# Queries and keys of the second block made with tokens on partitions, then transposed

## Chip, cores and metric

The kernel runs on one core of one Trainium2 chip. The metric is the device time of one execution in microseconds (us). TensorE is PE in the profile, VectorE DVE, ScalarE ACT, GpSimd POOL, and SP issues the weight transfers.

## What is computed

Two blocks of two layers each. The first block's layers are a hybrid mixer, a cross-attention over a memory and a SwiGLU network; the change leaves them alone. The second block takes the first one's output `x` [256 tokens, 1024] and a context of 256 tokens. Its layer has gated branches, one of which is a differential attention: 8 heads with two maps each, every map 64 wide, so queries and keys are 2 x 512 columns each of one large product with the layer's input. For each map of 64 columns `v` of a token, with gain `g`:

```
v = v * rsqrt(mean(v*v) + 1e-6) * g        # queries times 64**-0.5 as well
v = rotate(v, cos, sin)                    # not for the context
```

The rotation pairs columns d and d + 16 within each half of a map, one half by the token's row in a grid 64 wide, the other by its column. Then come scores, two softmaxes, their weighted difference, values, a norm, an output product and a feed-forward network with a small convolution. The context goes through one layer; of its second layer only keys and values are made. `x` goes through two layers and attends to its own tokens and the context's.

## The kernel before

Weights come as 908 units of [128, 1024] fp32, streamed by SP into four slots `raw` (L441). Each is split for exactness: ScalarE rounds it to `whi` (L1030, fp32r), POOL computes the rest `wlo = raw - whi` (L452), and TensorE adds three products (L473 to L475, or L499 to L501). ScalarE rounds the unit four places ahead as soon as TensorE has used the slot (`hi_part`), POOL follows, and SP refills `raw` when POOL is done. All five engines have their order written out by hand, with semaphores between them.

A chunk is 512 output columns over the full depth of 1024: four units. It goes to one of two halves of the PSUM tile `lin`, in one of two layouts. `feature_units` holds a piece of the weights still and streams the 256 tokens: 24 matmuls a unit, features on partitions. `token_units` holds 128 tokens of the input still and streams 512 weight columns: 12 matmuls a unit, tokens on partitions. `after={u: f}` lets TensorE do `f` behind unit u of the chunk.

`second_layer` on TensorE begins with the two chunks of the gated branch, then four chunks of queries (c = 0, 1) and keys (c = 2, 3), all with features on partitions, then two chunks of values with tokens on partitions. After unit 2 of chunk 0 comes `spatial_mix`, eight small fp32 matmuls on the gated branch, which waits for VectorE's statistics and scaling (L2065 to L2076). Four things are done for each chunk c while the next is being made:

- ScalarE evacuates it times the gain to `Z` (L1319, only with rotation) and writes its squares to `probs` (L1320); VectorE multiplies it by the cosines in place (L1933).
- TensorE swaps the partners of the rotation with a permutation matrix (`qk_partners`, L876); VectorE multiplies them by the sines into `probs` (L1476 under L1937), and adds.
- TensorE sums the squares over the partitions of each map (`qk_sums`, L888); ScalarE takes the root, VectorE the reciprocal (L1940), which for queries waits until the softmax.
- For keys TensorE spreads the reciprocals over the partitions (`qk_spread`, L900) and VectorE multiplies by them.

In the next chunk swap and sums stand after unit 0, the spread after unit 1. A pass of its own makes keys and values of the context for the second layer between the context's layer and the first of `x`, with chunks 2 and 3 in the same way. So 14 chunks of queries and keys are made: four in each of three calls, and two. L1476 and L1473 are helpers for every tensor_tensor and copy on VectorE; the tiles tell them apart. On the layer's start VectorE takes two products of the lambda row (L1476) and a sum (L2060).

## Time and profile before

| | us |
|---|---|
| median of 3 runs | 3021.04 |
| lowest, highest | 3016.26, 3025.08 |
| profiled execution | 3019.51 |
| its span | 3017.7 |
| TensorE matmuls busy | 2919.8 |
| POOL busy | 2179.8 |
| ScalarE, VectorE busy | 1515.8, 1097.9 |

Durations of matmul records overlap, since they are pipelined; what a chunk costs is read from stretches of the span. Mean granted clock of TensorE over the span: 0.973 of 2.4 GHz. The second block's layers take up the span from about 1342 us on: the context's layer, its extra pass from about 1863, the layers of `x` from about 1923 and 2478.

### The profile page before, as it was taken

The page shows a single profiled execution, that of the slowest core. Times are in us where ns is not written, and L with a number is a line of the kernel's source. Part 1 is how long each engine was busy: PE and PEld are TensorE (multiplying, and loading weights), DVE is VectorE, ACT ScalarE, POOL GpSimd, SP SyncE. Part 2 cuts the span into 40 slices and gives each one's busy share as a digit, 9 for nine tenths or more (in the row PEclk, how much of TensorE's full clock was granted, in tenths as well). Part 3 has the DMA queues.
Part 4 walks back from the last instruction along what each step waited for, and adds up shares of the span by engine and source line. Part 5 has one row for each costly group of instructions (what it writes and reads, how often), then busy time and mean ns, then how long its engine had stood idle before and what let it go on. Part 6 is the DMA issues. An engine that isn't in the chain of part 4 may idle for free.

```text
span 3017.7 us, 51871 instructions
## 1 busy us (share of the span) xinstructions
PE 2919.8 (97%) x21822; PEld 2692.0 (89%) x21822; DVE 1097.9 (36%) x1976; ACT 1515.8 (50%) x1999; POOL 2179.8 (72%) x912
## 2 busy tenths in 40 slices
PE   7998989999999999999999999999999999999999
PEld 7886969989877969989899999888899999889999
DVE  2411422122313331331552444326534342564433
ACT  4666454445665464454564444445654444465443
POOL 6667788886767688887667786665586866557677
PEclk9999999999999989999999999999999999999999
DMA  6445455555445455554445454533354554434454
GB/s 220 138 153 171 156 179 181 184 189 175 147 154 182 159 191 168 182 197 154 149 149 171 154 186 157 190 129 129 128 174 148 181 182 156 133 126 157 151 182 154
DMA packets 136521, 495.39 MB, mean 164 GB/s; under 512 B 15072, under 2 KB 17760, under 8 KB 135136
## 3 DMA queue, kind: packets, MB, share of 16 engines
q1 hardware_dynamic: 131904, 480.53, 47.6%
q10 hardware_dynamic: 4384, 11.54, 1.1%
q8 instruction: 172, 2.82, 0.4%
q14 instruction: 61, 0.50, 0.1%
HBM read 488.86 MB, written 3.15 MB: 163 GB/s over the span
## 4 chain that ended last, share of the span: by engine, by line
PE 83%; ACT 5%; DVE 4%; POOL 2%; DVEq 2%; issue 1%; ACTq 1%; DMA 1%; SPq 0%
PE lin L473 18%; PE lin L474 17%; PE lin L475 17%; PE aux L473 4%; PE aux L475 4%; PE aux L474 4%; POOL wlo L452 2%; PE lin L499 2%; PE aux L566 2%; PE lin L501 2%; PE lin L500 2%; ACT whi L1030 2%; PE aux L641 1%; PE aux L917 1%; PE lin L616 1%
## 5 line engine op out<-in xcount | busy, mean ns | idle before, releaser
L452 POOL TENSOR_TENSOR wlo<-raw,whi 128x1024 fp32r<-128x1024 f32 x908 | 2179.6, 2416 | 828.6 <-ACT whi L1030 827.4
L1030 ACT ACTIVATE whi<-raw 128x1024 fp32r<-128x1024 f32 x908 | 949.3, 1057 | 975.8 <-PE lin L475 713.8
L473 PE MATMUL lin<-in_hi,whi 128*128 128x256 f32 x3968 | 1146.5, 289 | 25.1 <-POOL wlo L452 22.3
L474 PE MATMUL lin<-in_lo,whi 128*128 128x256 f32 x3968 | 1128.0, 284 | 0.0
L475 PE MATMUL lin<-in_hi,wlo 128*128 128x256 f32 x3968 | 1127.6, 284 | 0.0
L473 PEld LDWEIGHTS lin<-in_hi,whi 128*128 128x128 f32 x3968 | 767.2, 193 | 60.8 <-issue 46.6
L474 PEld LDWEIGHTS lin<-in_lo,whi 128*128 128x128 f32 x3968 | 767.5, 193 | 0.8
L475 PEld LDWEIGHTS lin<-in_hi,wlo 128*128 128x128 f32 x3968 | 766.4, 193 | 0.0
L473 PE MATMUL aux<-br_hi,whi 128*128 128x256 f32 x880 | 249.1, 283 | 0.0
L474 PE MATMUL aux<-br_lo,whi 128*128 128x256 f32 x880 | 249.0, 283 | 0.0
L475 PE MATMUL aux<-br_hi,wlo 128*128 128x256 f32 x880 | 249.0, 283 | 0.0
L473 PE MATMUL lin<-br_hi,whi 128*128 128x256 f32 x768 | 224.8, 293 | 0.0
L474 PE MATMUL lin<-br_lo,whi 128*128 128x256 f32 x768 | 220.4, 287 | 0.0
L475 PE MATMUL lin<-br_hi,wlo 128*128 128x256 f32 x768 | 220.4, 287 | 0.0
L474 PEld LDWEIGHTS aux<-br_lo,whi 128*128 128x128 f32 x880 | 168.9, 192 | 0.0
L475 PEld LDWEIGHTS aux<-br_hi,wlo 128*128 128x128 f32 x880 | 168.9, 192 | 0.0
L473 PEld LDWEIGHTS aux<-br_hi,whi 128*128 128x128 f32 x880 | 168.9, 192 | 0.0
L1846 DVE TENSOR_SCALAR Z<-lin,par_all 128x256 f32<-128x256 f32 x132 | 62.7, 538 | 254.5 <-PE lin L475 254.5
L473 PEld LDWEIGHTS lin<-br_hi,whi 128*128 128x128 f32 x768 | 150.6, 196 | 5.3 <-issue 3.5
L474 PEld LDWEIGHTS lin<-br_lo,whi 128*128 128x128 f32 x768 | 150.7, 196 | 0.2
L475 PEld LDWEIGHTS lin<-br_hi,wlo 128*128 128x128 f32 x768 | 150.4, 196 | 0.0
L1476 DVE TENSOR_TENSOR Z<-Z,lin 128x512 f32<-128x512 f32 (+1 forms) x34 | 29.8, 876 | 293.4 <-ACT Z L1277 264.2
(247 smaller groups left out, 3688.4 us busy)
## 6 DMA issues: line engine op xcount, KB each, us to landing
raw<-in_wstream SPq DMA_DIRECT2D x908, 512.0 KB, 3.3
Z<-in_rel ACTq DMA_DIRECT2D x2, 1536.0 KB, 7.0
Z<-in_mem_t ACTq DMA_DIRECT2D x2, 1024.0 KB, 7.0
kv_store<-Z ACTq DMA_DIRECT2D x2, 1024.0 KB, 6.8
Z<-kv_store ACTq DMA_DIRECT2D x2, 1024.0 KB, 12.7
x<-in_x_t SPq DMA_DIRECT2D x1, 1024.0 KB, 4.9
Z<-in_ctx_t SPq DMA_DIRECT2D x1, 1024.0 KB, 4.9
out_x<-x SPq DMA_DIRECT2D x1, 1024.0 KB, 3.9
```

What stands on the lines that cost most here:

```text
L452: pool.tensor_tensor(wlo[s][:, :], raw[s][:, :], whi[s][:, :].bitcast(F32), ALU.subtract).then_inc(lo_pool, 1)
L473: pe.matmul(out, wh, xh, start=start, stop=False, skip_group_check=True)
L474: pe.matmul(out, wh, xl, start=False, stop=False, skip_group_check=True)
L475: return pe.matmul(out, wl, xh, start=False, stop=stop, skip_group_check=True)
L499: pe.matmul(out, xh, wh, start=start, stop=False, skip_group_check=True)
L500: pe.matmul(out, xh, wl, start=False, stop=False, skip_group_check=True)
L501: return pe.matmul(out, xl, wh, start=False, stop=stop, skip_group_check=True)
L566: mm = pe.matmul(square_sums(b)[:, tt:tt + 1], zt(tiles + k)[:, tt * P:(tt + 1) * P], ones[:, 0:1], start=(k == 0 and tt == 0), stop=(k == ...
L616: pe.matmul(lin[0:4, p, o:o + CH], c, wh[:, w], start=(k == 0), stop=False, skip_group_check=True)
L641: mm = pe.matmul(out, q[:, tt * P:(tt + 1) * P], k[:, 0:(tt + 1) * P], start=True, stop=True)
L1030: act.activation(whi[s][:, :], raw[s][:, :], ACT.Copy).then_inc(hi_ready, 1)
L1846: dve.tensor_scalar(o[c], u[c], w[c][:, 1:2], w[c][:, 3:4], ALU.mult, ALU.add)
```

## The change

All 14 chunks of queries and keys are made with tokens on partitions. ScalarE squares the chunk, VectorE sums the squares of each map (`qk_squares`). With rotation VectorE multiplies the chunk from PSUM by a table of cosines times gain into `y` (two instructions), its exchanged halves by a table of sines times gain into `probs` (four), and adds the two. It takes the reciprocal of the root, and for keys multiplies `y` by it. Without rotation queries are copied and keys are scaled, both from PSUM. After unit 2 of the next chunk TensorE transposes the eight [128, 128] pieces of `y`, and ScalarE evacuates them to the place where features on partitions were (`qk_out`), without rotation times the gain. Swaps, sums and spreads on TensorE go, and so does ScalarE's first evacuation.

The columns of a map come in another order (`ROTATED`), so that rotation partners are 32 columns apart. The tables with the gains are made by eight small instructions of VectorE at the start of a rotating layer (`qk_tables`); the gains come with the lambda row, whose transfer grows from 256 to 512 columns. The wait for the stored keys and values (`kv_sent`) moves from VectorE to ScalarE.

```diff
-C2 = dict(blk=0, perm=128, cos=256, sin=512)
+C2 = dict(cos=0, sin=128, turn=256)
 NC2 = 768
+ROTATED = np.arange(64).reshape(2, 2, 16).transpose(1, 0, 2).reshape(64)
...
-        qk = w[:, QK_COL:V_COL].reshape(D, 2, 2, NH, 64).swapaxes(2, 3).reshape(D, V_COL - QK_COL)
+        qk = w[:, QK_COL:V_COL].reshape(D, 2, 2, NH, 64).swapaxes(2, 3)[..., ROTATED].reshape(D, V_COL - QK_COL)
...
+        def qk_turn(c):
+            return zt(YB + 4 * (c % 2), 4)
+        def qk_table(c, sine, tt):
+            o = C2["turn"] + 256 * (c // 2) + 128 * sine + 64 * tt
+            return c2[:, o:o + 64]
...
+        qk_squares = small[:, 64:80]
...
-            def qk_partners(rotate):
-                if rotate:
-                    pe.wait_ge(qk_raw, t.next(qk_raw))
-                    if t.ahead(qk_done, 0):
-                        pe.wait_ge(qk_done, t.ahead(qk_done, 0))
-                    for h in range(2):
-                        mm = pe.matmul(aux[:, 2 + h, :], c2[:, C2["perm"]:C2["perm"] + P], zt(YB + 2 * h, 2), start=True, stop=True)
-                    mm.then_inc(qk_swap, 1)
-            def qk_sums(rotate, free=None):
-                qk_partners(rotate)
+            def qk_transposes(c, free=None):
+                pe.wait_ge(qk_turned, t.next(qk_turned))
                 if free:
                     pe.wait_ge(free, t.ahead(free))
-                pe.wait_ge(qk_sq, t.next(qk_sq))
                 if t.ahead(qk_done, 0):
                     pe.wait_ge(qk_done, t.ahead(qk_done, 0))
-                for j in range(4):
+                for h in range(4):
                     for tt in range(2):
-                        mm = pe.matmul(aux[:, 0, 4 * j + 2 * tt:4 * j + 2 * tt + 2], probs[:, j * T + tt * P:j * T + (tt + 1) * P],
-                                       c2[:, C2["blk"]:C2["blk"] + P:P // 2], start=True, stop=True)
-                mm.then_inc(qk_ss, 1)
+                        mm = pe.transpose(wide_aux(1 - c % 2)[:, h * T + tt * P:h * T + (tt + 1) * P],
+                                          qk_turn(c)[:, tt * CH + h * P:tt * CH + (h + 1) * P], ident)
+                mm.then_inc(qk_trans, 1)
                 t.skip(qk_done)
-            def qk_spread(c):
-                pe.wait_ge(qk_inverse, t.next(qk_inverse))
-                for j in range(4):
-                    for tt in range(2):
-                        for m in range(2):
-                            r = qk_scale(c)[:, 4 * j + 2 * tt + m:4 * j + 2 * tt + m + 1]
-                            mm = pe.matmul(aux[64 * m:64 * m + 64, j // 2, j % 2 * T + tt * P:j % 2 * T + (tt + 1) * P],
-                                           r.to_broadcast([P, 64]), ident, start=True, stop=True)
-                mm.then_inc(qk_wide, 1)
...
-                feature_chunk(0, after={2: spatial_mix})
+                token_chunk(0, after={2: spatial_mix})
                 for c in range(4):
-                    after = {0: lambda: qk_sums(rotate, ya_ready if c == 0 else None)}
-                    if c > 1:
-                        after[1] = lambda: qk_spread(c)
-                    if c < 3:
-                        feature_chunk((c + 1) % 2, after=after)
-                    else:
-                        token_chunk(0, after=after)
+                    token_chunk((c + 1) % 2, after={2: lambda: qk_transposes(c, ya_ready if c == 1 else None)})
...
-            normed_chunk()
-            feature_chunk(1, after={0: lambda: qk_sums(False), 1: lambda: qk_spread(2)})
-            token_chunk(0, after={0: lambda: qk_sums(False), 1: lambda: qk_spread(3), 3: latent_sums})
+            rms()
+            token_chunk(0, fresh=QUARTERS)
+            token_chunk(1, after={2: lambda: qk_transposes(2)})
+            token_chunk(0, after={2: lambda: qk_transposes(3), 3: latent_sums})
...
-            def qk_chunk(p, c, rotate, first=None, last=None):
-                yield from units(1)
-                if first:
-                    first()
-                yield from units(3)
-                units_done()
+            def qk_chunk(p, roots, last=None, end=None):
+                hi_part()
+                roots()
+                hi_parts(2)
                 if last:
                     last()
-                if rotate:
-                    gain = qk_gain[:, c // 2:c // 2 + 1]
-                    act.activation(zt(YB, 4), lin[:, p, :], ACT.Copy, scale=gain).then_inc(qk_raw, 1)
+                hi_part()
+                units_done()
+                if end:
+                    end()
                 act.activation(probs[:, 0:2 * CH], lin[:, p, :], ACT.Square).then_inc(qk_sq, 1)
 
             def qk_roots():
                 act.wait_ge(qk_ss, t.next(qk_ss))
-                root(qk_root, aux[:, 0, 0:16], qk_std, 1.0 / 64, 1)
-            def values_chunk(p, dst, first=None):
-                hi_parts(1)
-                if first:
-                    first()
-                evacuate(p, 3, dst)
+                root(qk_root, qk_squares, qk_std, 1.0 / 64, 1)
+            def qk_out(c, rotate, side=None):
+                act.wait_ge(qk_trans, t.next(qk_trans))
+                dst = three(zt(Q2 + 4 * c, 4), 4) if c < 2 else key_tiles(c - 2, (0 if rotate else 1) if side is None else side)
+                act.activation(dst, three(wide_aux(1 - c % 2), 4), ACT.Copy,
+                               scale=1.0 if rotate else qk_gain[:, c // 2:c // 2 + 1]).then_inc(qk_done, 1)
...
-                act.dma_start(zt(S2 + 4), a["lam"][l:l + 1, :].to_broadcast([P, T])).then_inc(sgu_landed, 16)
+                act.dma_start(zt(S2 + 4, 2), a["lam"][l:l + 1, :].to_broadcast([P, CH])).then_inc(sgu_landed, 16)
...
-                run(qk_chunk(0, 0, rotate, value_std, lambda: input_hi(br_hi[:, 0:4 * T], wide_aux(0))))
+                qk_chunk(0, value_std, None, lambda: input_hi(br_hi[:, 0:4 * T], wide_aux(0)))
+                v = VL if rotate else VC
                 for c in range(1, 4):
-                    run(qk_chunk(c % 2, c, rotate, qk_roots))
-                v = VL if rotate else VC
-                if rotate and l == 0:
-                    act.wait_ge(kv_sent, t.next(kv_sent, 32))
-                values_chunk(0, zt(v, 4), qk_roots)
+                    if c == 3 and rotate and l == 0:
+                        act.wait_ge(kv_sent, t.next(kv_sent, 32))
+                    qk_chunk(c % 2, qk_roots, lambda: qk_out(c - 1, rotate))
+                hi_part()
+                qk_roots()
+                hi_parts(2)
+                qk_out(3, rotate)
+                evacuate(0, 1, zt(v, 4))
...
+            def maps(ap, tt):
+                return ap[:, tt * CH:(tt + 1) * CH].rearrange("p (n d) -> p n d", d=64)
+            def part(ap, tt, s):
+                return ap[:, tt * CH:(tt + 1) * CH].rearrange("p (n s d) -> p n s d", s=2, d=32)[:, :, s]
+            def over_maps(ap, n):
+                return ap.unsqueeze(1).to_broadcast([P, 8, n])
+            def qk_tables(l):
+                gains = zt(S2 + 5)
+                for i in range(2):
+                    for sine in range(2):
+                        for tt in range(2):
+                            o = C2["sin" if sine else "cos"] + 64 * tt
+                            dve.scalar_tensor_tensor(qk_table(2 * i, sine, tt), c2[:, o:o + 64], (64 ** -0.5, 1.0)[i],
+                                                     gains[:, 128 * i + 64 * sine:128 * i + 64 * sine + 64], ALU.mult, ALU.mult)
+                settle()
+            def qk_chunk(c, rotate, between=None):
+                p = c % 2
+                z, y, b = lin[:, p, :], qk_turn(c), probs[:, 2 * CH:4 * CH]
+                scale = qk_scale(c).unsqueeze(2).to_broadcast([P, 16, 64])
                 if between:
                     between()
                 dve.wait_ge(qk_sq, t.next(qk_sq))
+                dve.tensor_reduce(qk_squares, probs[:, 0:2 * CH].rearrange("p (n d) -> p n d", d=64), AX.X, ALU.add).then_inc(qk_ss, 1)
+                if t.next(qk_done) > 2:
+                    dve.wait_ge(qk_done, t.ahead(qk_done, -2))
                 if rotate:
-                    dve.scalar_tensor_tensor(z, z, gain, over(cos, 4), ALU.mult, ALU.mult)
+                    for tt in range(2):
+                        tt_(maps(y, tt), maps(z, tt), over_maps(qk_table(c, 0, tt), 64), ALU.mult)
+                    for tt in range(2):
+                        for s in range(2):
+                            i = tt_(part(b, tt, s), part(z, tt, 1 - s), over_maps(qk_table(c, 1, tt)[:, 32 * s:32 * s + 32], 32), ALU.mult)
+                    i.then_inc(lin_free[p], 1)
                     settle()
-                if rotate:
-                    dve.wait_ge(qk_swap, t.next(qk_swap))
-                    tt_(turned, three(wide_aux(1), 4), over(sin, 4), ALU.mult)
+                    tt_(y, y, b, ALU.add)
                     settle()
                 dve.wait_ge(qk_std, t.next(qk_std))
-                i = dve.reciprocal(qk_scale(c), qk_root)
-                if c > 1:
-                    i.then_inc(qk_inverse, 1)
-                if rotate:
-                    tt_(dst, z, turned, ALU.add).then_inc(lin_free[p], 1)
-                else:
-                    dve.tensor_scalar(dst, z, gain, None, ALU.mult).then_inc(lin_free[p], 1)
-                settle()
-                if c > 1:
-                    dve.wait_ge(qk_wide, t.next(qk_wide))
-                    tt_(dst, dst, three(wide_aux(0), 4), ALU.mult)
-                settle().then_inc(qk_done, 1)
+                dve.reciprocal(qk_scale(c), qk_root)
+                settle()
+                if rotate and c > 1:
+                    tt_(y.rearrange("p (n d) -> p n d", d=64), y.rearrange("p (n d) -> p n d", d=64), scale, ALU.mult)
+                elif c > 1:
+                    tt_(y.rearrange("p (n d) -> p n d", d=64), z.rearrange("p (n d) -> p n d", d=64), scale, ALU.mult).then_inc(lin_free[p], 1)
+                elif not rotate:
+                    copy(y, z).then_inc(lin_free[p], 1)
+                settle().then_inc(qk_turned, 1)
...
+                    qk_tables(l)
...
-                    if c == 2 and rotate and l == 0:
-                        dve.wait_ge(kv_sent, t.next(kv_sent, 32))
```

## Rows read from the trace of the kernel before

**Rows 1.** the page, part 1: busy time, share of the span and instructions of each engine

```profile
PE 2919.8 (97%) x21822; PEld 2692.0 (89%) x21822; DVE 1097.9 (36%) x1976; ACT 1515.8 (50%) x1999; POOL 2179.8 (72%) x912
```

**Rows 2.** groups by form on TensorE (line engine op names shapes xcount | busy us, mean ns)

```profile
L888 PE MATMUL aux<-c,probs 128*128 128x2 f32 x224 | 25.9, 246 | 0.5 <-DVE br_lo L1476 0.5
L900 PE MATMUL aux<-c,qk_inv 128*64 128x128 f32 x256 | 15.7, 276 | 0.0
L876 PE MATMUL aux<-Z,c 128*128 128x512 f32 x32 | 15.2, 598 | 0.5 <-ACT Z L1319 0.5
```

**Rows 3.** windows (from:to, length, busy us of PE PEld DVE ACT POOL, PEclk, DMA share, GB/s)

```profile
1935.08:1945.99 10.91, 10.91 (x51) 9.02 (x49) 4.49 (x3) 5.16 (x5) 10.91 (x5) 1.00 0.76 272
1983.18:1994.78 11.60, 11.60 (x99) 11.60 (x99) 1.33 (x2) 5.03 (x6) 6.61 (x4) 1.00 0.38 123
1979.76:1983.18 3.42, 3.42 (x23) 2.46 (x21) 2.52 (x2) 1.31 (x2) 2.94 (x2) 1.00 0.62 205
2001.24:2003.13 1.89, 1.89 (x33) 1.72 (x32) 0.00 (x0) 1.06 (x1) 0.59 (x1) 1.00 0.01 2
2200.53:2202.25 1.72, 1.72 (x16) 1.72 (x17) 0.00 (x0) 1.70 (x2) 1.72 (x1) 1.00 0.83 293
1945.99:2025.52 79.53, 77.47 (x593) 70.57 (x592) 28.01 (x31) 32.94 (x36) 49.79 (x22) 1.00 0.43 144
2500.50:2577.97 77.47, 77.22 (x593) 70.51 (x592) 24.99 (x31) 32.94 (x36) 47.84 (x21) 1.00 0.42 142
1365.23:1436.13 70.90, 70.39 (x577) 67.48 (x576) 15.06 (x23) 29.33 (x32) 47.98 (x21) 1.00 0.46 154
```

**Rows 4.** groups by form on VectorE

```profile
L1476 DVE TENSOR_TENSOR probs<-aux,c 128x1024 f32<-128x1024 f32 x8 | 9.8, 1225 | 1.2 <-PE aux L876 0.9
L1476 DVE TENSOR_TENSOR br_lo<-aux,br_hi 128x256 fp32r<-128x256 f32 x32 | 13.6, 424 | 149.0 <-ACT br_hi L1087 149.0
L1476 DVE TENSOR_TENSOR Z<-Z 128x1024 f32<-128x1024 f32 x8 | 26.6, 3322 | 1.1 <-issue 0.5
L1476 DVE TENSOR_TENSOR Z<-Z,small 128x1024 f32<-128x1024 f32 x6 | 13.7, 2329 | 0.2
L2038 DVE TENSOR_REDUCE small<-probs 128x2 f32<-128x256 f32 x24 | 10.1, 422 | 2.0
L1940 DVE RECIPROCAL qk_inv<-qk_inv 128x16 f32<-128x16 f32 x14 | 3.5, 253 | 61.1 <-ACT qk_inv L1054 61.1
```

**Rows 5.** timeline of POOL and of VectorE (start us, us, engine line op names), 308 to 317

```profile
307.51 5.28 POOL L452 TENSOR_TENSOR wlo<-raw,whi 128x1024 fp32r<-128x1024 f32 x2 [0.48 <-ACT whi L1030]
...
310.51 3.37 DVE L1476 TENSOR_TENSOR Z<-Z 128x1024 f32<-128x1024 f32 x1
```

**Rows 6.** timeline of ScalarE, 1976.9 to 1985.5

```profile
1977.14 1.06 ACT L1030 ACTIVATE whi<-raw 128x1024 fp32r<-128x1024 f32 x1 [1.82 <-PE lin L475]
1979.10 1.02 ACT L1320 ACTIVATE probs<-lin 128x1024 f32<-128x1024 f32 x1
```

**Rows 7.** windows, as in Rows 3, at two waits of TensorE and behind them

```profile
1490.00:1492.60 2.60, 0.01 (x1) 0.00 (x0) 1.22 (x5) 2.44 (x6) 0.13 (x1) 1.00 0.00 0
1492.60:1496.00 3.40, 2.87 (x21) 2.30 (x22) 3.19 (x6) 1.01 (x2) 3.40 (x2) 1.00 0.13 13
2085.20:2088.10 2.90, 0.07 (x1) 0.00 (x0) 1.75 (x5) 2.44 (x6) 0.36 (x1) 1.00 0.01 3
2089.10:2092.50 3.40, 3.40 (x13) 2.05 (x10) 3.12 (x5) 0.34 (x1) 3.32 (x2) 0.50 0.40 131
```

**Rows 8.** timelines of POOL and VectorE, starts of the second block's rotating layers

```profile
1932.38 26.36 POOL L452 TENSOR_TENSOR wlo<-raw,whi 128x1024 fp32r<-128x1024 f32 x11 [5.01 <-ACT whi L1030]
...
1939.59 2.35 DVE L1476 TENSOR_TENSOR small<-par_all,c 128x1 f32<-128x1 f32 x1
1948.28 1.29 DVE L2065 BATCH_NORM_STATS2 small<-Z 128x6 f32<-128x512 f32 x2 [5.98 <-ACTq L1374]
...
2502.79 1.29 DVE L2065 BATCH_NORM_STATS2 small<-Z 128x6 f32<-128x512 f32 x2 [17.38 <-ACTq L1374]
```

More of the change, by code:

```diff
@@ L501, in token_product, with token_units @@
                 return pe.matmul(out, xl, wh, start=False, stop=stop, skip_group_check=True)
-            def token_units(p, src=None, after=()):
+            def token_units(p, src=None, after=(), fresh=()):
                 xh, xl = src or (in_hi, in_lo)
@@ L506, in token_units @@
                 for k0 in range(0, KD, 2):
+                    if k0 in fresh:
+                        pe.wait_ge(inputs_ready, t.next(inputs_ready))
                     wh, wl = next_unit()
@@ L1440, in _ @@
             rms(context, True)
-            run(qk_chunk(0, 2, False))
-            run(qk_chunk(1, 3, False, qk_roots))
+            qk_chunk(0, lambda: None)
+            latent_square(0)
+            qk_chunk(1, qk_roots, lambda: qk_out(2, False, 0))
             hi_part()
+            latent_square(1)
             qk_roots()
-            for q in range(3):
-                latent_square(q)
-                hi_part()
+            hi_part()
+            latent_square(2)
+            hi_part()
+            qk_out(3, False, 0)
             latent_square(3)
-            evacuate(0, 0, zt(VL, 4))
+            evacuate(0, 1, zt(VL, 4))
             norm_root(0, 1)
@@ L2212, in shape_constants @@
 def shape_constants():
-    i = np.arange(P)
     c1 = np.zeros((P, NC1), np.float32)
@@ L2269 @@
     taps = taps.reshape(L, 4, 2, NCH, 2, P).transpose(0, 5, 3, 2, 4, 1).reshape(L, P, 16 * NCH)
-    twice = [np.concatenate([v[n], v[n]], -1)[:, :, None] for n in ("q_norm_g_2", "k_norm_g_2")]
+    gains = [v[n][:, ROTATED] for n in ("q_norm_g_2", "k_norm_g_2")]
+    twice = [np.concatenate([g, g], -1)[:, :, None] for g in gains]
     par2 = np.concatenate([tiles(v["norm1_g_2"]), tiles(v["norm2_g_2"]), tiles(v["sgu_ln_g_2"])] + twice
@@ L2280 @@
         sgu_w=v["sgu_w_2"].transpose(0, 3, 1, 2).reshape(L * P, CH), sgu_b=v["sgu_b_2"].reshape(L, CH),
-        lam=np.concatenate([v[n] for n in ("lam_q1_2", "lam_q2_2", "lam_k1_2", "lam_k2_2")], -1),
+        lam=np.concatenate([v[n] for n in ("lam_q1_2", "lam_q2_2", "lam_k1_2", "lam_k2_2")]
+                           + [w for g in gains for w in (g, np.roll(g, 32, -1))], -1),
     )
```

34 lines of the change are left out of this document (13 added, 21 removed).

## Prediction

> **What bounds the kernel now.** I read first the busy line of the page [rows 1]: TensorE's matmuls fill 97% of the span, POOL 72%, the other two half or less. What TensorE is given to do is therefore the time, as long as nobody makes it wait. Next, who makes it wait, in the view of waits: in the part that changes only the spatial mix of one layer waits to speak of, and that stretch has 2.06 us idle in 79.53 [rows 3]. Then the price of each kind of TensorE work in that part, by form [rows 2] and by stretch [rows 3]. Last, the helpers, since the change moves work to VectorE, which shares something with POOL [rows 4, 5].
>
> **Price of a chunk.** A chunk of four units takes TensorE 10.91 us when made with tokens on partitions and 11.60 with features on partitions; the second starts behind a group of small matmuls, which costs it 0.08 [rows 3]. So 0.69 a chunk, 0.155 a unit.
>
> **What leaves TensorE.** The swaps (L876), square sums (L888) and spreads (L900) count 32, 224 and 256 matmul records [rows 2], at 4, 16 and 32 a group: 8, 14 and 8 groups. A swap with a sum takes 3.42 us [rows 3]; halved, 1.71 each. A spread takes 1.89. Together 22 x 1.71 + 8 x 1.89 = 52.7 us, all on the path, as TensorE is full there.
>
> **What comes.** Eight transposes a chunk, 14 chunks. Sixteen of the same kind take 1.72 us [rows 3]; eight 0.86, and 0.15 for the matmuls to start again behind them: 14 x 1.01 = 14.1. Bounds: 0.8 and 1.9 a group (the dearest small group in [rows 3]).
>
> **Check by stretch.** From the first query chunk to the last key chunk's end plus one value chunk the second and third layer calls take 79.53 and 77.47 us, the context 70.90 [rows 3]. Anew, each is five token chunks (54.55), a spatial mix (1.71, as a sum) and four transpose groups (4.04): 60.3. That gives 19.2, 17.2 and 10.6. The context's pass for the second layer's keys loses two sums and two spreads and turns two chunks: 3.4 + 3.8 + 1.3, restarts 0.5, less 2.0, is 7.0. Sum 54.0. The parts give 52.7 + 14 x 0.69 - 14.1 = 48.3; the stretches add the idle time of before (2.06, 0.25 and 0.51, busy time against length [rows 3]) and some 0.1 us of restart behind each of the 30 small groups, 3. **Gross saving 54.0 us**, if TensorE never waits.
>
> **Where it will wait.** TensorE asks for a chunk's transposes when three units of the next are done: 3 x 2.73 = 8.2 us after the chunk's own end, T. What must happen by then, from T: ScalarE rounds one unit, then squares; in the trace, where T is 1979.76 - 2.88 = 1976.9, the rounding starts at T + 0.2 and the squares at T + 2.2, with an evacuation of 1.0 between that now goes [rows 6]. So the squares run from 1.2 to 2.2. VectorE sums 1024 columns: 1.2, from 0.42 for 256 [rows 4]. Then two products of 512 and four of 256 columns. These read one operand from PSUM; 1024 columns take 1.23 and 256 take 0.42 [rows 4], so 2 x 0.6 + 4 x 0.33 with their overlap: 2.6. At T + 6.0 the sum y + b wants to start, with everything in SBUF.
> This is the weak step. Instructions of VectorE with both inputs in SBUF are dear in this trace: 3.32 us against 1.23 for the same 1024 columns [rows 4]. One is shown [rows 5]: it starts while POOL works, and ends 1.08 us after that POOL instruction (307.51 + 5.28 = 312.79) has ended. POOL's takes 2.40 [rows 8]. So they take turns. POOL's instructions follow ScalarE's rounding of the units at T + 0.2, 2.9 and 5.7, hence run from 1.4, 4.1 and 6.8. The sum lands in the second, waits to 6.5, ends at 7.6; with the reciprocal (0.25 [rows 4]) and drains, ready at 8.0. **Query chunk 1: no wait.** A key chunk has a second such instruction, the scaling. POOL has taken its turn at 7.6 and holds to 9.9; the scaling ends at 11.0. **Key chunks: 2.9 us each.** Chunk 0 starts 1.3 later, as ScalarE and VectorE first do the gating tile; its sum comes at 7.3, meets POOL's third (to 9.2), ready at 10.7: **2.5 us**. Each layer that rotates: 2.5 + 0 + 2.9 + 2.9 = 8.3; two: 16.6. In the context and its second pass there is no rotation and the scaling reads PSUM: ready by T + 6.7, no wait. Bounds for one chunk: 0 (nothing waits for POOL; the chain ends by 8.8) and 5.5 (one turn more).
>
> **The tables.** Eight small products a rotating layer, both inputs in SBUF, before the gates' statistics. In the first such layer POOL runs eleven instructions without a gap from 1932.38 [rows 8], and VectorE's single-column product there takes 2.35 us: a turn each. From 1942.3 five tables wait a turn (2.5 each, to 54.4); then POOL runs dry, because ScalarE waits for the statistics with its rounding behind it, and the rest is quick. The statistics start at 55.0 for 48.28 [rows 8], the mix at 58.4, where TensorE is ready at 54.2: 4.2 us idle (the 2.06 of before is in the stretch's saving already). In the last layer VectorE has 17.38 us idle there [rows 8], which hides six or seven turns: 0. Bounds 0 and 8 over both.
>
> **The clock.** A wait of 2.9 us is followed by 3.4 us at 0.50 of the clock, that is 1.2 GHz; another of 2.6 is not [rows 7]. Half of 3.4 at half speed costs 1.6 to 1.7. Of the seven waits above (4.2, 2.5 twice, 2.9 four times) I charge six: 9.8. Bounds 0 and 16.
>
> **Costed at nothing.** ScalarE's new evacuations (1.0 a chunk) fall between the third and fourth unit, with units already rounded ahead; without that lead each would cost its 1 us. The wait for kv_sent moves to ScalarE, with the transfer long landed. The lambda row grows from 1 to 2 KB a partition behind two transfers as large. Weights, SP's queue and POOL's work are the same: POOL needs 2.40 a unit, TensorE 2.73.
>
> **Sum.** The profiled execution took 3019.5 us (span 3017.7), 1.5 under the median of 3021.0. 3019.5 - 54.0 + 16.6 + 4.2 + 9.8 = 2996.1 against its own time; for a median 1.5 more, **2997**.
>
> **What a page adds.** Sixteen transposes at 2200.53 ran at clock 1.00 between dense matmuls [rows 3]. The Trainium skill, "TensorE: Matmul & The Clock Gate", Part 4, says that transpose-mode work does not count as busy for the clock. By that rule a drop would follow each of the 14 groups; nothing in [rows 3] shows it for 1.72 us between full stretches. What it would give is the second rival.
>
> **Rivals.**
> *No turns.* The new SBUF instructions slip between POOL's: y + b and scaling 1.2 each. Chunk 0 and the keys wait 0.7, the tables nothing, no clock drop: 3021 - 54 + 4 + 2 = 2973. For: POOL idles 0.48 before its instructions [rows 5]. Against: the six instructions of the scaling's form average 2.33, the eight of the sum's 3.32 [rows 4]. 0.15.
> *A clock drop at every group*, or a turn more for chunk 1 and in the last layer's tables: 14 x 1.65 instead of 9.8, or 2 x 2.5 + 3 + 3 drops: about 3010. For: groups of low activity follow waits. Against: [rows 3]. 0.15.
> *The rotation itself waits in turn.* If the six products with a table in SBUF were held by POOL as well, nine turns would stand in a chunk's chain. POOL has at most four instructions in hand before TensorE stalls (four slots), so the chain ends at 1.4 + 4 x 2.4 + 6.2 = 17.2, a wait of 9. Eight chunks: 72, clock 13, tables 4: 3021 - 54 + 89 = 3056, slower. It decides from about 6 us of loss a chunk. Against: products of that form take 1.23 whether POOL runs or not [rows 4]. 0.06.
> *TensorE's saving is no saving* because units come no faster (POOL or transfers bound): 3015 to 3021. Against: a token chunk takes 10.91 with POOL at work all through it [rows 3]. 0.05.
>
> **Numbers.** Forecast 0.59. About 0.3% (9 us) is what a measurement of this kernel can tell from no change: the forecast, the first and the second rival lie below 3012. The range leaves out the third and fourth and the ends of the others: 2975 to 3012. Faster 0.86, same 0.08, slower 0.06.
>
> **What would show it.** In the profile after: three or more lines gone (swaps, sums, spreads), 112 transposes at some 0.11 us pace; token chunks at 10.9; idle of TensorE before the transposes near 16.6 us in 6 or 7 pieces, released by VectorE's scaling or reciprocal; VectorE's y + b at 1.5 to 3.5 us each; a wait of 4 us before the first rotating layer's mix; six short stretches at half clock. The step most likely wrong is the chain on VectorE; if TensorE's idle time there is under 5 us the first rival holds, if over 60 the third.

## The result, and the profile after

| | before | after |
|---|---|---|
| median, us | 3019.42 (4 runs, 3016.26 to 3025.08) | 2991.08 (4 runs, 2988.91 to 2997.06) |
| profiled execution, its span | 3019.51, 3017.7 | 2991.71, 2989.9 |
| mean granted clock | 0.973 | 0.971 |

The ratio is 0.9911, 95% interval 0.9896 to 0.9925: 28 us off, where 24 were forecast (2997 from a median of 3021.04; range 2975 to 3012). The page's busy line after the change, beside [rows 1]:

```profile
PE 2873.9 (96%) x20750; PEld 2627.2 (88%) x20750; DVE 1149.2 (38%) x2030; ACT 1521.4 (51%) x2005; POOL 2189.0 (73%) x912
```

TensorE has 46 us less to do, VectorE 51 more, POOL 9 more. In the groups by form the swaps, sums and spreads of [rows 2] are gone and 112 transposes have come (L890; line 900 is now the spatial mix). The idle time before them stands behind the second bar.

```profile
L890 PE MATMUL aux<-c,Z 128*128 128x128 f32 x112 | 16.8, 299 | 16.1 <-DVEq L1965 16.1
L900 PE MATMUL aux<-Z 128*128 128x128 f32 x48 | 7.4, 321 | 3.3 <-DVE Z L2092 3.3
```

Now windows (columns as in [rows 3]). First a token chunk of the context's layer, with the restart behind a group; a group of eight transposes; then the stretches that answer to the last three of [rows 3], context, first and last layer that rotate: 59.92 for 70.90, 78.04 for 79.53, 70.42 for 77.47.

```profile
1387.36:1398.35 10.99, 10.99 (x52) 9.05 (x51) 2.70 (x3) 5.83 (x7) 8.82 (x5) 1.00 0.47 161
1398.35:1399.14 0.79, 0.79 (x9) 0.79 (x8) 0.00 (x0) 0.53 (x1) 0.79 (x1) 1.00 1.03 342
1365.65:1425.57 59.92, 59.92 (x291) 50.19 (x289) 17.85 (x25) 33.08 (x36) 49.25 (x21) 1.00 0.54 182
1926.44:2004.48 78.04, 66.94 (x289) 55.17 (x288) 44.30 (x58) 32.81 (x36) 55.05 (x22) 0.91 0.46 153
2479.35:2549.77 70.42, 62.14 (x291) 51.05 (x289) 37.73 (x52) 33.04 (x36) 53.70 (x21) 0.98 0.48 164
```

The context's layer saves 11.0, as TensorE is never idle there. The layers that rotate would save as much and more, and give it back in idle time (11.1 and 8.3 us: length less PE busy) and in clock (0.91 and 0.98). The view of waits names the two lines that are new:

```profile
PE aux L890 <- DVEq L1965: 16.1, 6, 2.9
PE aux L900 <- DVE Z L2092: 3.3, 1, 3.3
```

Six waits before the transposes of chunks 0, 2 and 3 of both layers, none before chunk 1's, none in the context. What holds VectorE is seen in the timeline of a key chunk (start us, us), VectorE's rows first, then two of POOL's instructions:

```profile
1975.49 1.28 DVE L1468 TENSOR_TENSOR Z<-lin,c 128x512 f32<-128x512 f32 x2
1976.69 1.41 DVE L1468 TENSOR_TENSOR probs<-lin,c 128x256 f32<-128x256 f32 x4
1978.19 1.53 DVE L1468 TENSOR_TENSOR Z<-Z,probs 128x1024 f32<-128x1024 f32 x1
1979.80 0.25 DVE L1957 RECIPROCAL qk_inv<-qk_inv 128x16 f32<-128x16 f32 x1
1980.12 2.90 DVE L1468 TENSOR_TENSOR Z<-Z,qk_inv 128x1024 f32<-128x1024 f32 x1
```

```profile
1976.23 2.41 POOL L462 TENSOR_TENSOR wlo<-raw,whi 128x1024 fp32r<-128x1024 f32 x1 [0.33 <-ACT whi L1016]
1978.93 3.01 POOL L462 TENSOR_TENSOR wlo<-raw,whi 128x1024 fp32r<-128x1024 f32 x1 [0.29 <-ACT whi L1016]
```

POOL's first ends at 1978.64 and the sum y + b 1.08 us later; its second ends at 1981.94 and the scaling, asked for at 1980.12, 1.09 later, at 1983.03. The turn is taken both ways: POOL's second instruction, which started while the sum was at work, took 3.01 us, the one before it 2.41. The six products that read one operand from PSUM (`lin`) run at their own pace beside POOL.

**Where the time went.** For each profiled execution I count three things from the first matmul to the last: TensorE's idle pieces of over 1 us, what stretches at 0.50 of the clock cost (half their length), and the rest.

| | idle | half clock | rest | median of runs |
|---|---|---|---|---|
| before | 53.5 | 80.2 | 2862.3 | 3019.42 |
| after | 70.7 | 87.0 | 2810.4 | 2991.08 |

So 52.0 us of work left TensorE, 17.2 came back as idle time and 6.8 as clock; what remains is the 27.9 by which the stretch from first to last matmul is shorter. The rest is the steady part: in the experiments below in which TensorE's work is that of the changed kernel it lies between 2808 and 2815, while the half-clock column moves by up to 20 us, most of it in stages that no edit touches (the first block alone has from 44 to 56 us of it).

### The profile page after: what moved, and what is told of

Its sections match the earlier page's. It is cut to its first block, busy times and chain, and to the rows that moved or that the text cites. A ratio compares the mean times of both kernels' runs of the same rounds, so it can differ in the third digit from the quotient of the medians.

```text
span 2989.9 us, 49777 instructions
## 1 busy us (share of the span) xinstructions
PE 2873.9 (96%) x20750; PEld 2627.2 (88%) x20750; DVE 1149.2 (38%) x2030; ACT 1521.4 (51%) x2005; POOL 2189.0 (73%) x912
## 4 chain that ended last, share of the span: by engine, by line
PE 82%; DVE 6%; ACT 5%; DVEq 2%; POOL 2%; issue 1%; ACTq 1%; DMA 1%; SPq 0%
PE lin L483 16%; PE lin L484 16%; PE lin L485 16%; PE aux L483 4%; PE aux L485 4%; PE aux L484 4%; PE lin L509 3%; PE lin L511 3%; PE lin L510 3%; ACT whi L1016 2%; PE aux L578 2%; POOL wlo L462 2%; PE aux L908 1%; PE aux L653 1%; DVE Z L1468 1%
## 5 line engine op out<-in xcount | busy, mean ns | idle before, releaser
L483 PE MATMUL lin<-in_hi,whi 128*128 128x256 f32 x3520 | 1018.1, 289 | 24.5 <-POOL wlo L462 22.9
L484 PE MATMUL lin<-in_lo,whi 128*128 128x256 f32 x3520 | 1001.4, 284 | 0.0
L485 PE MATMUL lin<-in_hi,wlo 128*128 128x256 f32 x3520 | 1001.1, 284 | 0.0
L483 PEld LDWEIGHTS lin<-in_hi,whi 128*128 128x128 f32 x3520 | 681.2, 194 | 59.5 <-issue 46.1
L484 PEld LDWEIGHTS lin<-in_lo,whi 128*128 128x128 f32 x3520 | 681.5, 194 | 0.6
L485 PEld LDWEIGHTS lin<-in_hi,wlo 128*128 128x128 f32 x3520 | 680.6, 193 | 0.0
L509 PE MATMUL lin<-whi,in_hi 128*128 128x512 f32 x464 | 186.3, 402 | 0.1
L511 PE MATMUL lin<-whi,in_lo 128*128 128x512 f32 x464 | 182.5, 393 | 0.0
L510 PE MATMUL lin<-wlo,in_hi 128*128 128x512 f32 x464 | 182.5, 393 | 0.0
```

Of the source, the lines that this page charges most:

```text
L483: pe.matmul(out, wh, xh, start=start, stop=False, skip_group_check=True)
L484: pe.matmul(out, wh, xl, start=False, stop=False, skip_group_check=True)
L485: return pe.matmul(out, wl, xh, start=False, stop=stop, skip_group_check=True)
L509: pe.matmul(out, xh, wh, start=start, stop=False, skip_group_check=True)
L510: pe.matmul(out, xh, wl, start=False, stop=False, skip_group_check=True)
L511: return pe.matmul(out, xl, wh, start=False, stop=stop, skip_group_check=True)
```

## Experiments

Theory: on VectorE an instruction with both operands in SBUF takes turns with POOL's (it waits for POOL's to end, and POOL's for it), whatever its size; that makes the six waits and the mix's wait. Rivals: the chain of instructions is too long by itself; or transposes lower the clock. Each diff is against the changed kernel; L numbers are lines of the kernel that ran. Ratios are to the kernel before, with 95% intervals.

**1. The sums in PSUM** (`e1_sums_in_psum`). The same arithmetic; `b` lies in a free half of `aux`, and for keys so does the sum that the scaling reads.

```diff
-                z, y, b = lin[:, p, :], qk_turn(c), probs[:, 2 * CH:4 * CH]
+                z, y, b = lin[:, p, :], qk_turn(c), wide_aux(1 - c % 2)
-                    tt_(y, y, b, ALU.add)
+                    tt_(b if c > 1 else y, y, b, ALU.add)
...
-                    tt_(y.rearrange("p (n d) -> p n d", d=64), y.rearrange("p (n d) -> p n d", d=64), scale, ALU.mult)
+                    tt_(y.rearrange("p (n d) -> p n d", d=64), b.rearrange("p (n d) -> p n d", d=64), scale, ALU.mult)
```

> The sine products go to PSUM instead of SBUF, and for keys the sum too, so that neither the sum nor the scaling has both inputs in SBUF; number and columns of VectorE's instructions stay. Theory (VectorE's instructions with two SBUF inputs take turns with POOL): sums and scalings take about 1.2 us each instead of 1.9 and 2.9, TensorE's idle time before the transposes falls from 16.1 to about 3.5 us (0.5 for chunk 0, 0.6 for each key chunk), the half-clock stretches of this part fall from five to one or two, and the time from 2991 to about 2972. Rival (the chain on VectorE is simply too long, whoever else works): nothing changes, 2991.

Median 2971.0, ratio 0.985 (0.9833 to 0.9866), 20 us under the changed kernel by the medians, 18 by the ratios. Its view of waits, and two rows of VectorE's timeline in a key chunk, which POOL's instruction from 1970.32 to 1972.70 overlaps:

```profile
PE aux L890 <- DVEq L1965: 4.6, 6, 1.1
```

```profile
1969.59 1.23 DVE L1468 TENSOR_TENSOR aux<-Z,aux 128x1024 f32<-128x1024 f32 x1
1971.22 1.22 DVE L1468 TENSOR_TENSOR Z<-aux,qk_inv 128x1024 f32<-128x1024 f32 x1
```

The scaling went from 2.90 to 1.22 us, the waits from 16.1 to 4.6, and none of the six was followed by a half-clock stretch. As many instructions, in the same order: it is not the chain's length.

**2. The transposes one unit later** (`e3_after_unit_3`), the sums left in SBUF.

```diff
-                    token_chunk((c + 1) % 2, after={2: lambda: qk_transposes(c, ya_ready if c == 1 else None)})
+                    token_chunk((c + 1) % 2, after={3: lambda: qk_transposes(c, ya_ready if c == 1 else None)})
...
-                    qk_chunk(c % 2, qk_roots, lambda: qk_out(c - 1, rotate))
+                    qk_chunk(c % 2, qk_roots)
+                    qk_out(c - 1, rotate)
...
+                evacuate(0, 1, zt(v, 4))
                 qk_out(3, rotate)
-                evacuate(0, 1, zt(v, 4))
```

ScalarE's evacuation of the transposes so comes behind its squares; on VectorE nothing is edited.

> The transposes of a chunk stand after unit 3 of the next chunk instead of unit 2, 2.7 us later, and ScalarE evacuates them after its squares; no instruction's operands change. Theory: the sums keep their 1.5 to 3 us and the scalings 2.9, but the chain, ready 8.4 to 10.9 us after the chunk's end, now meets a deadline of 10.9: TensorE's idle time there falls from 16.1 to under 1.5 us, four half-clock stretches go, 2970. Rival (the wait only moves: the evacuation comes later and holds up the next chunk's buffer, the first scores or the units' rounding): 2985 to 2995 with TensorE idle elsewhere.

Median 2969.96, ratio 0.9844 (0.983 to 0.9859). Of the waits at L890 one of 0.2 us is left, though by form VectorE's instructions are dearer than in the changed kernel (1909 and 2902 ns there):

```profile
L1469 DVE TENSOR_TENSOR Z<-Z,probs 128x1024 f32<-128x1024 f32 x8 | 21.6, 2694 | 0.7
L1469 DVE TENSOR_TENSOR Z<-Z,qk_inv 128x1024 f32<-128x1024 f32 x4 | 11.8, 2938 | 0.3
```

The turns cost only because TensorE asked 2.7 us too early. Two quite different edits give about the same: 18 and 20 us by the ratios.

**3. Two columns** (`e4_tiny_sbuf`, `e5_tiny_psum`). A product of 2 columns, needed by nobody, behind chunk 1's reciprocal and ahead of the signal; in the second kernel its first operand is `wide_aux(0)[:, 0:2]`, in PSUM.

```diff
+                if rotate and c == 1:
+                    tt_(small[:, 84:86], qk_squares[:, 0:2], qk_squares[:, 0:2], ALU.mult)
```

> One more VectorE product of two columns, both inputs in SBUF, behind the reciprocal of query chunk 1 in the two rotating layers (its result is not used). Theory (a turn, whatever the size): it takes about 2 us instead of 0.2, chunk 1's transposes, which had no wait, wait about 2 us in each layer; 4 us more, up to 7.5 with half-clock stretches: 2995 to 2999. Rival (its own size counts): 0.2 us each, 2991.

> The same added product of two columns as in the run with the tiny product, but one of its two operands comes from PSUM. Theory (turns with POOL for an instruction with both operands in SBUF): about 0.1 to 0.3 us each instead of 1.83, no wait before chunk 1's transposes, so five waits of 2.4 to 3.0 us and the short one at line 890, some 16 us in all, time 2989 to 2993. Rival (any further product in that place costs what the other one did, its own start and end): about 1.8 us again, with waits of 1.6 us before chunk 1's transposes.

VectorE's product and POOL's instruction beside it, first with both operands in SBUF, then with one in PSUM:

```profile
1962.39 1.84 DVE L1468 TENSOR_TENSOR small<-small 128x2 f32<-128x2 f32 x1
1961.22 2.99 POOL L462 TENSOR_TENSOR wlo<-raw,whi 128x1024 fp32r<-128x1024 f32 x1 [0.31 <-ACT whi L1016]
```

```profile
1965.22 0.16 DVE L1468 TENSOR_TENSOR small<-aux,small 128x2 f32<-128x2 f32 x1
1964.05 5.36 POOL L462 TENSOR_TENSOR wlo<-raw,whi 128x1024 fp32r<-128x1024 f32 x2 [0.31 <-ACT whi L1016]
```

The same two columns, the same place in the chain, and POOL at work in both: 1.84 us, ending 0.02 behind POOL's end, against 0.16, with 1.68 of POOL's instruction (the first of the two in its row, which ends at 1967.06) still to run. The second rotating layer has the same two numbers within 0.01. With the first TensorE got two more waits, of 1.61 us each, before chunk 1's transposes (line 890: 19.0 us in 8), with the second none (15.8 in 6). The times do not show it: 2990.49 (0.9919, 0.9898 to 0.994) and 2985.86 (0.9897, 0.9872 to 0.9922). The intervals overlap, and the first, forecast at 2995 to 2999, is no slower than the changed kernel: its profiled execution had 8.5 us less of half clock, by chance as far as I can see, and its two new waits were followed by none. The price of the turn is shown by the rows, that of the wait only in the trace.

The Trainium skill, "SBUF — State Buffer", section on the two sides of SBUF, says that a VectorE instruction with two SBUF inputs and a GpSimd instruction that reads SBUF exclude one another for the whole instruction. These rows agree, down to 2 columns, and so does experiment 1 for the remedy.

**4. The tables in four instructions** (`e2_tables_split`): two of 128 columns before the statistics, two behind chunk 0's sum, instead of eight of 64 before.

```diff
-            def qk_tables(l):
+            def qk_tables(i):
                 gains = zt(S2 + 5)
-                for i in range(2):
-                    for sine in range(2):
-                        for tt in range(2):
-                            o = C2["sin" if sine else "cos"] + 64 * tt
-                            dve.scalar_tensor_tensor(qk_table(2 * i, sine, tt), c2[:, o:o + 64], (64 ** -0.5, 1.0)[i],
-                                                     gains[:, 128 * i + 64 * sine:128 * i + 64 * sine + 64], ALU.mult, ALU.mult)
+                for sine in range(2):
+                    o, g = 128 * sine, gains[:, 128 * i + 64 * sine:128 * i + 64 * sine + 64]
+                    two = lambda c: c2[:, c:c + 128].rearrange("p (t d) -> p t d", t=2)
+                    dve.scalar_tensor_tensor(two(C2["turn"] + 256 * i + o), two(o), (64 ** -0.5, 1.0)[i],
+                                             g.unsqueeze(1).to_broadcast([P, 2, 64]), ALU.mult, ALU.mult)
                 settle()
...
-                    qk_tables(l)
+                    qk_tables(0)
...
                 for c in range(4):
                     lo_parts(4)
                     qk_chunk(c, rotate, gating_lo if c == 0 else None)
+                    if rotate and c == 0:
+                        qk_tables(1)
```

> Two table instructions before the gates' statistics instead of eight (the key tables are made after chunk 0, when VectorE is idle; each instruction does both halves of the tokens). Theory (each costs one POOL instruction of 2.4 us there): in the first rotating layer the statistics start as soon as ScalarE has the gates, TensorE's wait before the spatial mix falls from 3.3 to about 2.1 us, what VectorE's two scalings leave; 1.2 us less, 2.8 if the half-clock stretch goes as well: 2988 to 2990. Rival (the wait comes from the longer lambda transfer or from ScalarE): 3.3 stays, 2991.

Median 2991.93, 0.9906 (0.9882 to 0.9931): no gain to be seen where 2988 to 2990 was expected, and of the mix's wait of 3.3 us 2.4 stayed. VectorE's timelines at the start of the first rotating layer show why. The changed kernel, in which POOL ran without a gap from 1912.79 to 1934.10:

```profile
1922.63 11.96 DVE L1932 SCALAR_TENSOR_TENSOR c<-c,Z 128x64 f32<-128x64 f32 x8
1934.66 1.29 DVE L2081 BATCH_NORM_STATS2 small<-Z 128x6 f32<-128x512 f32 x2
...
1936.90 1.00 DVE L2092 TENSOR_SCALAR Z<-Z,small 128x512 f32<-128x512 f32 x2
```

and the kernel with four tables, in which it ran to 1945.95:

```profile
1929.36 4.63 DVE L1931 SCALAR_TENSOR_TENSOR c<-c,Z 128x128 f32<-128x128 f32 x2
1935.49 1.29 DVE L2080 BATCH_NORM_STATS2 small<-Z 128x6 f32<-128x512 f32 x2 [1.51 <-ACTq L1359]
...
1938.75 0.17 DVE L2087 RECIPROCAL small<-small 128x2 f32<-128x2 f32 x1 [1.65 <-ACT small L1040]
1938.99 4.74 DVE L2091 TENSOR_SCALAR Z<-Z,small 128x512 f32<-128x512 f32 x2
```

TensorE is ready for the mix at 1934.67 and at 1941.38, so against it the statistics start 5.9 us earlier. But VectorE waits 1.65 for ScalarE's root, and the two scalings, which have one wide input, in SBUF, take 4.74 instead of 1.00: now POOL works beside them. In the changed kernel POOL had run dry, because ScalarE held its roundings back behind the late statistics. The stall moved from the tables to the scaling.

**5. The gated half in PSUM** (`e10_gate_in_psum`, `e11_u3_tables_again`, `e12_gate_alone`), to test that. All three have the transposes behind the fourth unit. The eleventh adds the split tables; the tenth adds them and this edit; the twelfth this edit alone.

```diff
-                evacuate(1, 4, zt(GB + 4, 4), func=ACT.Gelu_apprx_tanh)
+                evacuate(1, 4, wide_aux(1), func=ACT.Gelu_apprx_tanh)
...
-                    last = dve.tensor_scalar(vt, vt, small[:, 40 + 2 * tt:41 + 2 * tt], small[:, 14 + tt:15 + tt],
+                    last = dve.tensor_scalar(vt, wide_aux(1)[:, tt * CH:(tt + 1) * CH], small[:, 40 + 2 * tt:41 + 2 * tt], small[:, 14 + tt:15 + tt],
```

The statistics read `wide_aux(1)` too.

> Transposes after the fourth unit and tables in two groups, and in addition ScalarE writes the gated branch's second half to PSUM, from where VectorE takes the statistics and the scaling before the mix. With the tables split, the statistics of the first rotating layer start 5.9 us earlier than before the split, but the two scaling instructions (one input, in SBUF) take 4.7 us instead of 1.0, as POOL now runs beside them. Theory (an instruction with its one wide input in SBUF takes a turn with POOL too; from PSUM it doesn't): the two take 1.0 to 1.3 us, the mix of the first rotating layer waits 0 instead of 2.4 us, and the time is 2.4 us less, or 4.1 with the half-clock stretch behind the wait, than the same kernel without this edit in this call. Rival (they are slow for another reason, such as the write to SBUF or ScalarE's late root): still over 4 us, wait still 2.4.

> Transposes after the fourth unit and tables in two groups once more, on the chip of the other runs of this call, to compare them with: 2960 to 2968 us, the mix waits 2.4 us, the two scaling instructions take 4.7 us.

> Transposes after the fourth unit, all eight tables before the statistics as in the changed kernel, and the gated half in PSUM. Theory: here the tables alone set the mix, as POOL has run dry when the scaling comes: the statistics start no earlier, the scaling takes 1.0 to 1.3 us as without the edit, the mix still waits 3.1 to 3.5 us, and the time is that of the fourth unit alone, 2966 to 2973 us. Rival (the edit helps by itself, by a shorter chain): the wait is under 2.4 us here too.

The scaling in the kernel with the tables split, with this edit too, and with this edit alone:

```profile
1932.20 4.72 DVE L2092 TENSOR_SCALAR Z<-Z,small 128x512 f32<-128x512 f32 x2
```

```profile
1933.76 1.53 DVE L2092 TENSOR_SCALAR Z<-aux,small 128x512 f32<-128x512 f32 x2
```

```profile
1940.79 1.53 DVE L2093 TENSOR_SCALAR Z<-aux,small 128x512 f32<-128x512 f32 x2
```

| transposes behind unit 4, and | scaling, us | mix waits, us | median | ratio |
|---|---|---|---|---|
| tables split (eleventh) | 4.72 | 2.4 | 2964.58 | 0.9821 (0.9806 to 0.9836) |
| tables split, half in PSUM (tenth) | 1.53 | 0 | 2962.05 | 0.9809 (0.9789 to 0.9829) |
| half in PSUM alone (twelfth) | 1.53 | 3.9 | 2966.7 | 0.982 (0.9801 to 0.984) |

In the tenth POOL works all through the scalings; in the twelfth it starts at 1941.54, so it works beside the second alone, and each takes 0.80 as in the tenth. So from PSUM they cost 0.53 more than the 1.00 from SBUF with POOL still, and no turn (1.0 to 1.3 was expected), and alone the edit makes the wait 0.6 longer, not shorter. With both edits the last new wait is gone. So the wait needed both: tables and scaling. The times stand in the order forecast, but the intervals overlap; the waits carry the verdict. (The twelfth's profiled execution, with a granted clock of 0.95 outside its half-clock stretches, took 10 us over its median; only its wait is used.)

**6. Combined versions** (`e6_psum_tables`, `e7_all`, `e8_u3_tables`), made of the edits of experiments 1, 2 and 4 as shown: 1 and 4; 1, 2 and 4; 2 and 4.

> Sums in PSUM and the tables in two groups; transposes stay after the third unit. Theory: 2968 to 2972, six short waits of 0.6 to 1.1 us before the transposes, none followed by a stretch at half clock, and 2.4 us before the first rotating layer's mix. Rival (the tables' wait matters through the clock behind it): the half-clock stretch behind the mix goes with the shorter wait, 1.7 us more off, 2966 or less.

> Sums in PSUM, transposes after the fourth unit instead of the third, and the tables halved in number and in two groups, together. Theory: the first two take away the same waits (16.1 us of idle and five stretches at half clock), so they do not add: 2964 to 2970, no wait before any transposes, the mix of the first rotating layer waits 2.4 us. Rival (each of the two also saves something of its own, such as the work or the order around it): savings of 20 and 21 us would add to some 2950.

> Transposes after the fourth unit, and the tables in four instructions, two of them behind chunk 0's sum; the sums stay in SBUF. Theory: VectorE's sums and scalings still stand their turns (2.7 to 2.9 us on average, several of them), and nobody waits for them: time as with the fourth unit alone, less 0.9 us of the mix's wait, 2966 to 2971. Rival (VectorE's longer chain comes back as a wait of the heads or of the next chunk's evacuation): over 2975.

| | line 890 waits | idle | half clock | rest | median | ratio |
|---|---|---|---|---|---|---|
| sums in PSUM | 4.6 | 54.4 | 75.1 | 2815.3 | 2971.0 | 0.985 |
| unit 4 | 0.2 | 53.8 | 81.9 | 2810.7 | 2969.96 | 0.9844 |
| sums in PSUM, tables split | 4.1 | 54.4 | 73.4 | 2812.8 | 2966.37 | 0.9829 (0.9806 to 0.9853) |
| all three | 0 | 52.9 | 85.3 | 2808.1 | 2964.95 | 0.9824 (0.9796 to 0.9851) |
| unit 4, tables split | 0 | 52.5 | 76.8 | 2811.1 | 2960.25 | 0.9809 (0.9774 to 0.9845) |

Sums in PSUM and the later place do not add: both take away the same waits (16.1 us of idle time). The first and the third came out 2 and 6 us faster than the ranges given for them; the third is the kernel of the eleventh run too, which had 2964.58, so 4 us of spread lie between two sets of runs of one kernel. The three combined versions cannot be told apart. All are 25 to 31 us under the changed kernel, so the 24 us that it gave back can be had without losing what it saved; the simplest, the transposes behind the fourth unit, has 20 of these by the ratios.

**7. Each group of transposes four times over** (`e9_transposes_x4`), in the version with unit 4 and the tables split. It tests the rival of the clock.

```diff
-                for h in range(4):
+                for h in 4 * [0, 1, 2, 3]:
```

> The version with the transposes after the fourth unit and the tables in two groups (median 2960.25 us), with each group of eight transposes issued four times over, 32 instead of 8, 14 groups. Theory (a transpose costs its own pace of 0.1 us and nothing else): 14 x 24 x 0.099 = 33 us more, 2991 to 2996, and every group runs at clock 1.00 and so does what follows it, as no wait stands ahead of it. Rival (a stretch of transposes lowers the clock; a page of the notes says that transpose-mode work does not count as busy): the groups now last 3.2 us each, so that a stretch at 0.50 of the clock is met in most of the 14, at least 1.7 us each: 24 us more again, some 3017.

Two groups of 32, in the context's and in a rotating layer, and what follows each:

```profile
1390.45:1393.86 3.41, 3.41 (x33) 3.41 (x32) 1.15 (x1) 1.97 (x2) 3.07 (x2) 1.00 0.64 239
1393.86:1397.30 3.44, 3.44 (x18) 2.88 (x17) 0.07 (x1) 1.48 (x2) 0.36 (x1) 1.00 0.57 194
1971.58:1974.99 3.41, 3.41 (x33) 3.41 (x33) 3.41 (x2) 1.98 (x2) 3.41 (x2) 1.00 0.53 169
1974.99:1985.98 10.99, 10.99 (x52) 9.05 (x50) 7.79 (x10) 4.41 (x5) 7.10 (x4) 1.00 0.39 133
```

The clock stays at 1.00, through the groups and behind them. In no group of the 14 does a half-clock stretch begin, and behind one only, 6 us later, after the 32 small matmuls of the pass's sums (L578), where the kernel before had one as well, and the second kernel of experiment 3 and that of experiment 4 too, with groups of eight. Were transposes idle time for the clock, 3.41 us of them should do what waits of 2.4 to 2.9 us did in 17 of 24 cases (below); they did in none of 14. Median 3003.37, ratio 0.9949 (0.9932 to 0.9965), 43 us over the version that it is made from and 39 over its repeat in experiment 5, where the theory said 33 and the rival 57: outside both ranges, 2991 to 2996 and about 3017. In the profiled executions the difference is 39.2: the rest rose by 32.3, as forecast, idle and half clock by 3.4 each in other places.

## Why the prediction was right

- **What leaves and what comes.** Forecast 54.0 us gross, of which 2.06 were idle time of before; measured 52.0 of work, the same. By stretch: context 11.0 (forecast 10.6). For the two layers that rotate 60.3 us of work each was forecast; matmuls busy less half of the stretches at 0.50 is 60.1 and 60.4. The context's extra pass 10.9 (forecast 7.0), of which 3.4 is a half-clock stretch of 6.8 us that only the execution before had; the windows of the pass, before and after, show it in the clock, 0.94 and 1.00:

```profile
1863.15:1923.57 60.42, 60.42 (x423) 55.01 (x421) 19.31 (x36) 26.17 (x32) 34.67 (x15) 0.94 0.35 115
```

```profile
1854.13:1903.70 49.57, 49.57 (x244) 41.79 (x245) 21.64 (x34) 28.03 (x34) 34.67 (x15) 1.00 0.42 143
```

- **The transposes.** Forecast 0.86 a group and 0.15 for the restart; measured 0.79, and a chunk behind a group 10.99 for 10.91, so 0.87 instead of 1.01: 2 us too dear over 14. As the whole came out right, something else was 2 us too cheap. In the context's stretch five chunks and four groups leave 1.89 for the mix, where 1.71 was forecast, which is 0.5 us over three layers; the rest is not located.
- **The chain on VectorE,** the step called weakest: 16.6 us in six pieces forecast, 16.1 in six measured. For the key chunk above the chunk's own end, T in the prediction, is 1971.99; the sum was to start at T + 6.0 and end at T + 7.6, the scaling to end at T + 11.0, with POOL's turns ending at T + 6.5 and T + 9.9. The rows have T + 6.2, 7.7, 11.0, 6.65 and 9.95. That VectorE's instruction ends 1.08 us behind the POOL instruction that held it, read off one pair of [rows 5], is what made this exact. Experiments 1 to 3 show that it is the turn and not the length. Chunk 1 of each layer waits nothing, as forecast.
- **The tables.** Forecast five turns and a wait of 4.2; the eight instructions took 11.96 us with five turns, and the wait was 3.3. In the last layer nothing, as forecast.
- **The clock.** Six stretches for 9.8 us forecast; behind the seven waits five were seen (8.5 us), and the whole program's half-clock cost rose by 6.8, as the extra pass had lost 3.4 and other places gained 1.7. This term was a guess within bounds, and its closeness is in part luck: in the changed kernel and experiments 3 and 4, 17 of 24 waits of 2.4 to 2.9 us before transposes were followed by a stretch of 3.4 at 0.50, and 7 were not. Three, in the order hit, missed, hit:

```profile
1983.11:1986.51 3.40, 3.40 (x13) 3.11 (x14) 0.00 (x0) 1.02 (x1) 2.13 (x1) 0.57 0.50 160
2529.81:2533.21 3.40, 3.40 (x19) 2.98 (x20) 0.00 (x0) 1.03 (x1) 2.16 (x1) 1.00 0.48 164
1999.70:2003.10 3.40, 3.40 (x13) 2.82 (x12) 0.00 (x0) 1.02 (x1) 1.61 (x1) 0.50 0.45 163
```

- **Costed at nothing.** ScalarE's evacuations, the moved wait for `kv_sent` and the longer lambda row appear in no wait of TensorE; the context's stretch is 59.92 busy of 59.92.
- **The rivals.** No turns fell: the sums and scalings average 1.9 and 2.9 us. What it forecast, 2973, is near what experiment 1 gave by taking the turns away. The clock drop at every group fell: neither 0.79 nor 3.41 us of transposes, among dense matmuls, lowered the clock here. The Trainium skill, "TensorE: Matmul & The Clock Gate", Part 4, says that transposes do not count as busy for the clock; these groups do not bear that out for fp32 and up to 3.41 us. Longer groups were not tried. (Each transpose is one record in the trace and each of the mix's fp32 matmuls two, 48 for 24, so the transposes do seem to run in a mode of their own.) The rotation itself does not wait: its six products take 2.6 us with POOL beside them. And TensorE's saving was a saving.

Against the profiled executions the sum gave 2996.1 and the time was 2991.7. The 4.4 between them are 1.5 of idle time (17.2 for 20.8 less 2.06) and 3.0 of clock (6.8 for 9.8), within rounding. The half-clock cost moves by more than that between executions, so the mechanism is confirmed by the waits and the work, and the last few us of the agreement are luck.

## What to carry to other kernels

When work moves from TensorE to a helper, price each of the helper's instructions by where its operands lie and by what runs on POOL beside it, not by its columns alone; an operand in a free piece of PSUM took the turn away, at no cost for the sums and for 0.5 us more on the two scalings of the gate. Then set the chain's end against the moment at which TensorE asks: one unit later in the order was worth 20 us without an edit to the chain on VectorE. And when a stall is shortened, look at which instruction behind it will then meet the engine that the stall had kept still.

## What was not expected of the hardware

- A product of 2 columns took 1.84 us, and tables of 64 columns 2.4 each, four in a row behind one of 2.15, against 0.21 for the last three with POOL still: what the turn costs is what POOL's instruction has left to run.
- Some instructions with one wide input take a turn too: two `tensor_scalar` of 512 columns from SBUF to SBUF took 4.7 us beside POOL, 1.00 with POOL still, and 1.53 with the input in PSUM. Not all of that kind do. The two statistics took 1.29 in both timelines of experiment 4, with POOL still in the first and at work in the second. The sum of the squares, from SBUF to SBUF as well, takes its 1.22 while POOL works from 1973.49 to 1975.90, and in 11 of the 14 chunks it runs wholly beside POOL at 1.22:

```profile
1974.36 1.22 DVE L1943 TENSOR_REDUCE small<-probs 128x16 f32<-128x1024 f32 x1 [6.13 <-ACT probs L1305]
```

- Waits of the same length at the same place in two layers (2.68 us before chunk 3's transposes, in the second kernel of experiment 3) were followed by a half-clock stretch in one and not in the other. Of the waits under 1.7 us before transposes (14 in the kernels with sums in PSUM and with the product in SBUF) none was. What decides for the longer ones stays open.
- The half-clock cost of a whole profiled execution went from 73 to 94 us over nine kernels, most of it in stages that none of the edits touch. So a gain of under 5 us cannot be read from a few times here; it has to be read from the waits.
